# Forget-gate logits of a hybrid decoder layer: one stationary tile with high and low weights in separate columns, two passes for three

## The reference, cut to what matters

```python
h    = modulate(rms_norm(x, g_pre_mix), sh1, sc1)          # (512, 2048)
proj = h @ w_in                                            # (512, 5128)
u_lru, u_gate, q, k, v, f_logit = split(proj)              # f_logit: (512, 8)
log_f = log_sigmoid(f_logit + b_forget)
F = cumsum(log_f, axis=tokens)                             # attention bias: F_t - F_s
```

## Time and profile before

| what | us |
|---|---|
| median of 3 runs | 2231.93 |
| lowest and highest of the 3 | 2231.49, 2233.23 |
| the profiled execution, its own time | 2231.94 |
| span of the profiled execution, first to last instruction | 2229.5 |
| PE busy over the span | 2128.8 |
| DVE busy over the span | 1619.8 |
| ACT busy over the span | 799.9 |
| POOL busy over the span | 163.8 |

### The profile page before, as it was taken

The page is one execution under the profiler, slowest core; times in us unless marked ns, Lnnn a source line. Parts: engine busy times, 40 slices in busy tenths (PEclk is TensorE's granted clock), DMA queues, the critical chain, the costliest instruction groups (busy, mean ns, idle before and its releaser), DMA issues.

```text
span 2229.5 us, 25155 instructions
## 1 busy us (share of the span) xinstructions
PE 2128.8 (95%) x9081; PEld 1694.0 (76%) x9081; DVE 1619.8 (73%) x1777; ACT 799.9 (36%) x1024; POOL 163.8 (7%) x145
## 2 busy tenths in 40 slices
PE   3779999999999999999999999999999999999997
PEld 3557778887777777787787787787787787787876
DVE  7998597868685665766766867767767767767756
ACT  4113622222454244433433433333433333433432
POOL 3441140000021000000000000000000000000000
PEclk8889999999999999999999999999999999999999
DMA  9875457876435653323223323323233223223333
GB/s 331 285 244 157 148 158 259 292 270 200 155 119 179 222 204 95 95 85 123 94 85 114 102 85 104 104 92 103 95 101 105 94 88 119 94 85 113 104 126 138
DMA packets 178461, 321.42 MB, mean 144 GB/s; under 512 B 12600, under 2 KB 47528, under 8 KB 176096
## 3 DMA queue, kind: packets, MB, share of 16 engines
q1 hardware_dynamic: 172576, 303.12, 41.7%
q0 software_dynamic: 3568, 16.95, 2.2%
q10 hardware_dynamic: 2256, 0.53, 0.1%
HBM read 312.15 MB, written 8.42 MB: 144 GB/s over the span
## 4 chain that ended last, share of the span: by engine, by line
PE 69%; DVE 18%; issue 7%; ACT 5%; DVEq 0%; ACTq 0%; DMA 0%
PE pair L743 9%; PE pair L745 9%; PE pair L744 9%; DVE acc L1282 7%; PE pair L767 7%; PE pair L768 7%; PE pair L769 7%; PE bank L458 4%; PE bank L460 4%; PE bank L459 4%; PE bank L470 3%; PE bank L468 3%; PE bank L469 3%; ACT w_hi L1124 2%; DVE op_lo L1576 2%
## 5 line engine op out<-in xcount | busy, mean ns | idle before, releaser
L1609 DVE TENSOR_TENSOR yg<-yg,pair 128x1024 f32<-128x1024 f32 x240 | 289.8, 1218 | 317.1 <-PE pair L769 317.1
L743 PE MATMUL pair<-h_hi,w_lo 128*128 128x512 f32 x1024 | 406.2, 397 | 5.1 <-issue 5.1
L745 PE MATMUL pair<-h_hi,w_hi 128*128 128x512 f32 x1024 | 405.5, 396 | 0.0
L744 PE MATMUL pair<-h_lo,w_hi 128*128 128x512 f32 x1024 | 405.1, 396 | 0.0
L767 PE MATMUL pair<-w_hi,op_lo 128*128 128x512 f32 x840 | 334.0, 398 | 4.2 <-DVE op_lo L1576 4.1
L768 PE MATMUL pair<-w_lo,op_hi 128*128 128x512 f32 x840 | 333.4, 397 | 0.0
L769 PE MATMUL pair<-w_hi,op_hi 128*128 128x512 f32 x840 | 332.5, 396 | 0.0
L743 PEld LDWEIGHTS pair<-h_hi,w_lo 128*128 128x128 f32 x1024 | 192.4, 188 | 52.2 <-issue 5.9
L745 PEld LDWEIGHTS pair<-h_hi,w_hi 128*128 128x128 f32 x1024 | 192.7, 188 | 47.1
L744 PEld LDWEIGHTS pair<-h_lo,w_hi 128*128 128x128 f32 x1024 | 192.7, 188 | 46.7 <-issue 0.2
L458 PE MATMUL bank<-h_hi,w_lo 128*128 128x512 f32 x512 | 214.3, 419 | 14.2 <-POOL h_lo L1753 10.7
(11 more groups left out here) (255 smaller groups left out, 2866.7 us busy)
## 6 DMA issues: line engine op xcount, KB each, us to landing
raw<-in_w_ada_dram SPq DMA_DIRECT2D x128, 512.0 KB, 4.7
w_raw<-in_w_ff_dram SPq DMA_DIRECT2D x128, 512.0 KB, 3.8
raw<-in_w_ff_dram SPq DMA_DIRECT2D x128, 512.0 KB, 4.5
raw<-in_w_in_dram SPq DMA_DIRECT2D x82, 512.0 KB, 4.8
gst<-in_w_ada_dram SPq DMA_DIRECT2D x64, 512.0 KB, 6.0
raw<-in_w_out_dram SPq DMA_DIRECT2D x32, 512.0 KB, 3.9
x_tok<-in_x_dram SPq DMA_DIRECT2D x4, 1024.0 KB, 8.4
xr<-in_x_dram POOLq DMA_DIRECT2D x4, 1024.0 KB, 7.1
```

The lines of the kernel that those rows point to most:

```text
L743: pe.matmul(b, lo[:, cols], h_hi[:, kt, :], start=(kt == 0), stop=False)
L744: pe.matmul(b, hi[:, cols], h_lo[:, kt, :], start=False, stop=False)
L745: last = pe.matmul(b, hi[:, cols], h_hi[:, kt, :], start=False, stop=(kt == KT - 1))
L1609: dve.tensor_tensor(y, y, pairs[2 + (i + r) % 2][:, :, :], ALU.subtract if i == 6 else ALU.add).then_inc(product_read, 1)
```

## The change

The two tiles `wf_hi` and `wf_lo` become one tile `wf`: high weights in columns 0 to 7, low weights in columns 32 to 39, zeros elsewhere. PE multiplies the tile by `h_lo` and then by `h_hi`, 32 matmuls in place of 48; rows 0 to 7 of the bank then hold the high weights' products and rows 32 to 39 those of the low weights (by both parts of the activations). ACT copies rows 32 to 39 out of PSUM, DVE adds the bias, the high rows and the copied low rows in one instruction, and ACT goes on with the absolute value. `forget()` moves behind unit 52's `lo_part` and ada blocks on DVE. POOL zeroes one tile in place of two.

```diff
-        *_, wf_hi, wf_lo = overlay(("pad3", [P, 128 * 256], F32), ("wf_hi", [P, KT, P], F32R), ("wf_lo", [P, KT, P], F32R))
+        *_, wf = overlay(("pad3", [P, 128 * 256], F32), ("wf", [P, KT, P], F32R))
...
+        F_HI, F_LO = slice(0, HEADS), slice(32, 32 + HEADS)
...
                         pe.wait_ge(wf_lo_ready, 1)
                         for kt in range(KT):
-                            last = feature_major([banks[0]], (wf_hi[:, kt, :], wf_lo[:, kt, :]), h_hi, h_lo, kt, KT, range(1))
+                            pe.matmul(banks[0][:, :], wf[:, kt, :], h_lo[:, kt, :], start=(kt == 0), stop=False)
+                            last = pe.matmul(banks[0][:, :], wf[:, kt, :], h_hi[:, kt, :], start=False, stop=(kt == KT - 1))
                         last.then_inc(f_done, 1)
...
                 if e == 30:
 
                     act.wait_ge(wf_in, 16)
-                    act.wait_ge(wf_zero, 2)
-                    act.activation(wf_hi[:, :, 0:HEADS], wf_raw[:, :, :], ACT.Copy).then_inc(wf_hi_ready, 1)
+                    act.wait_ge(wf_zero, 1)
+                    act.activation(wf[:, :, F_HI], wf_raw[:, :, :], ACT.Copy).then_inc(wf_hi_ready, 1)
...
                 if e == 6 * 8 + 3:
 
                     act.wait_ge(f_done, 1)
-                    act.wait_ge(bf_in, 16)
                     act.wait_ge(ssq_done, CT)
-                    act.activation(ut[0:HEADS, 0, :], banks[0][0:HEADS, :], ACT.Identity, bias=bf[:, :]).then_inc(f_read, 1)
+                    act.activation(ut[0:HEADS, 1, :], banks[0][F_LO, :], ACT.Copy).then_inc(f_low, 1)
                     act.wait_ge(f_read, 1)
...
                 if e == 31:
                     dve.wait_ge(wf_hi_ready, 1)
-                    dve.tensor_tensor(wf_lo[:, :, 0:HEADS], wf_raw[:, :, :], wf_hi[:, :, 0:HEADS].bitcast(F32),
+                    dve.tensor_tensor(wf[:, :, F_LO], wf_raw[:, :, :], wf[:, :, F_HI].bitcast(F32),
                                       ALU.subtract).then_inc(wf_lo_ready, 1)
                 if e == 6 * 8 + 3:
+                    dve.wait_ge(f_low, 1)
+                    dve.wait_ge(bf_in, 16)
+                    dve.scalar_tensor_tensor(ut[0:HEADS, 0, :], banks[0][F_HI, :], bf[:, :], ut[0:HEADS, 1, :],
+                                             ALU.add, ALU.add).then_inc(f_read, 1)
+                if e == 6 * 8 + 4:
                     forget()
...
             pool.wait_ge(ssq_done, CT)
-            pool.memset(wf_hi[:, :, :].bitcast(F32), 0.0).then_inc(wf_zero, 1)
-            pool.memset(wf_lo[:, :, :].bitcast(F32), 0.0).then_inc(wf_zero, 1)
+            pool.memset(wf[:, :, :].bitcast(F32), 0.0).then_inc(wf_zero, 1)
```

More of the change, by code:

```diff
@@ L223, in hybrid_layer @@
         q_copied, k_copied, v_copied = sem("q_copied"), sem("k_copied"), sem("v_copied")
-        wf_zero, wf_hi_ready, wf_lo_ready, f_done, f_read, f_exp = (
-            sem(n) for n in ("wf_zero", "wf_hi_ready", "wf_lo_ready", "f_done", "f_read", "f_exp"))
+        wf_zero, wf_hi_ready, wf_lo_ready, f_done, f_low, f_read, f_exp = (
+            sem(n) for n in ("wf_zero", "wf_hi_ready", "wf_lo_ready", "f_done", "f_low", "f_read", "f_exp"))
         nf_ready, nf_stored, nfm_ready = sem("nf_ready"), sem("nf_stored"), sem("nfm_ready")
```

## The result

The changed kernel took 2234.26 us (median of 20 runs, 2231.94 to 2238.0), the kernel before 2231.67 us in the same comparison (20 runs, 2227.79 to 2233.23). The medians are 2.6 us apart; the ratio is 1.0015, 95% interval [1.0009, 1.0021], which is 3.3 us slower, give or take 1.3. I had forecast 2230.5 and a range up to 2232.6, so the prediction was wrong, and in its sign too.

The account below looks back on a forecast made before the run. The prediction took PE to bound this part. 3.64 us saved in the forget pass less a 2.2 us stall ahead of unit 56 gave 1.4 us off 2231.9, so 2230.5 us, range 2227.8 to 2232.6.

Parts of the forecast that it names:

- The pass: On PE, ahead of unit 48: 16 dropped matmuls at 0.2275 us each save 3.64 us.
- The hand-over: ACT's copy to DVE's new 0.68 us instruction and back to ACT, done near 498.5: free, as `hi_part(52)` starts at 500.2.
- the sum: The prediction's worked-out timeline and total: 3.64 us saved less a 2.2 us stall ahead of unit 56, 1.4 us less.
- `forget()` one unit later: On DVE: `forget()` runs from 505.6 to 519.95; no stall at unit 53, slack 2.3 us in place of 5.7.
- The gate into group 7: PE's wait for `row_std` ahead of unit 56: late loads of unit 55's and 57's weights stall PE 2.2 us.
- The gate gets later than before: Rival, ahead of unit 56: 8.3 us loads delay the root to 547.9, 2.5 us behind unit 56's old start; 2234.4 us, chance 0.12.
- The whole pass is gained: Rival, ahead of unit 56: unit 57's weights land by 539.1, so all 3.64 us stays; 2228.3 us, chance 0.20.

Follow-up runs that it names:

- row job early: Changed kernel with PE's row job moved from behind unit 49 to behind unit 48: 2230.49 us, ratio 0.9997 against the kernel before.
- root late: Kernel before with ten small copies on ACT ahead of the square root of the row statistics: 2233.78 us, ratio 1.0012.

## Why the prediction was wrong

**The pass.** Right: 3.64 us forecast, 3.63 measured, and all of it reaches the attention when nothing stalls. With the one tile used twice in a row a matmul took 7.29 / 32 = 0.228 us, as before.

**The hand-over.** Right. The new instruction took 0.74 us (0.68 taken), and `hi_part(52)` began at 498.75 - 485.59 = 13.16 us behind the start of the pass, 13.14 by the sum. It is free: with `forget()` at its old place the hand-over is still there, and no part of the gain is missing.

**`forget()` one unit later: the step that failed.** The prediction said that DVE "does the low part (about 1.15) and two ada blocks (3.11, rows 6), and starts `forget()` at 505.6". It took the blocks of unit 52 at the duration of unit 51's, and those have no wait. It gave the 5.35 us of idle time before the low part its cause, and never asked whether the first instruction behind it had a wait of its own. That instruction waits for PE's row job behind unit 49, and the job comes 5.6 us after the end of unit 48 that releases the low part. Before, `forget()` stood ahead of this wait and covered it. `forget()` then took 14.36 us as in the sum (14.35), but it began 22.8 us behind the start of the pass where the sum has 18.5, and the 2.3 us of slack at unit 53 became a stall of 1.8. The row job early shows it: with the wait gone, so is the stall.

**The gate into group 7.** Right in place, and near in size where its inputs were those of the sum: 2.2 us forecast, 2.9 with the row job early. In the changed kernel the 2.0 and 2.7 come near it by luck: the gate opened 3.6 us later against the start of the pass than in the sum (60.5 us, sum 56.9), and PE, held up at unit 53, came later too. The rows of before carried the slow loads: the reload by POOL ran again, and the loads beside it took up to 8.6 us (8.4 for unit 55's weights) with the row job early. The Trainium skill ("DMA: Bandwidth & Descriptors", section "Anatomy of one DMA") fits the time of DMAs that GpSimd issues; taken over to these, which SP issues, it gives an estimate of 3.2 us for such a load. The traces agree where the load is alone (3.4 us for the first behind `forget()` in the changed kernel) and not in company (6.9 for unit 55's weights there, 8.4 with the row job early).

**The price of a stall: a term that the prediction did not have.** It charged a stall its own length. The profiles show about 1.6 us more behind each stall of 2 us and over at the gate, up to the first score. Up to the last score the 1.6 us at the gate is made up, because the heads then kept the full clock. So this term alone does not make the changed kernel slower than forecast. What does is the failed step. In the second profile of the changed kernel, with the full clock behind unit 53, the kernel is 1.2 us behind the kernel before at the last score where the sum had it 1.4 ahead. Of these 2.6 us, 2.1 is the stall at unit 53 with the restart and 0.5 the longer stall at the gate. In the first profile low clock behind unit 53 came on top.

**The rivals.** "The gate gets later than before" had the right sign and the wrong cause. It wanted loads of 8.3 us for the weights of both unit 55 and unit 57; in the changed kernel they took 6.9 and 4.8 us. The gate moved because `forget()` started 4.3 us later than in the sum. "The whole pass is gained" is what the kernel with `forget()` at its old place does, and there for a reason that I did not name: DVE's long stretch moves forward with the pass. The forecast held DVE's chain to be where it was ("the 3.6 us that PE gained it has not gained"). That was not a property of the pass but of the move.

What stays open: why the heads keep the full clock once PE has idled at the gate, and why the executions of the changed kernel spread over 6 us. Low clock behind unit 53, in one of two profiles, would do a part of it. The two profiles also differ in other stretches at half the clock, near 305 us and behind the heads. Which of them came in the runs that were not profiled is not on record.

## What to carry to other kernels

When a long piece of work is moved past other work on an in-order queue, list the wait of every instruction that it is moved behind, and not their durations alone. A wait that the long piece covered until now becomes its start. An instruction that opens a buffer used in turn (here the one that reads `acc_init`) is the place to look. A saving on the bounding engine is kept whole only if the chain that feeds it next starts earlier as well, so place such a chain as early as its input allows.

## What the runs showed of the hardware

A stall of TensorE can be followed by a loss that no list of waits shows. In the kernel before with the root late, 2.6 us of idle time, in a stretch without another for over 200 us, was followed by half the clock for 3.4 us, 1.6 us lost. The matmul's own length shows it (0.63 us drawn in place of 0.39), and so does the granted clock of a narrow window; in the share of busy time it counts as work.

The length of the stall does not decide it alone. In the eleven profiles, half the clock followed each of the five idle times of 2.0 to 3.5 us at the gate. It followed one of five of 1.8 us at unit 53, and none of 0.9 to 1.4 us. It followed 4 of 11 of 2.1 us near 302 us, and 5 of 11 of 2.2 us at the start of the heads.

Those five at the heads are just the profiles in which PE had not idled at the gate, some 50 us earlier. In the six in which it had, for 1.2 to 3.5 us, the heads ran at the full clock and took 1.6 us less. So what one stall costs in clock can be given back at the next one. Read right behind the stall at the gate, the loss came out 1.6 us too large here; it should be read again behind the next place where PE idles anyway. No run shows why the heads behave so.
